# Row exchange of the rotary embedding by DMA instead of a product, with the sine product on GpSimd

## The reference, cut to what matters

```
def apply_rope(x, cos, sin):
    x1, x2 = jnp.split(x.astype(jnp.float32), 2, axis=-1)
    c = cos[None, :, None, :]
    s = sin[None, :, None, :]
    return jnp.concatenate([x1 * c - x2 * s, x2 * c + x1 * s], axis=-1).astype(x.dtype)
```

## Time and profile before

| | us |
|---|---|
| runs (three) | 2032.0, 2032.95, 2035.33 |
| median | 2032.95 |
| profiled execution, its own time | 2036.08 |
| profiled execution, span of the trace | 2034.3 |
| TensorE busy (matmul) | 1961.6, 96% of the span |
| VectorE busy | 1085.8, 53% |
| ScalarE busy | 986.6, 48% |
| GpSimd busy | 753.6, 37% |

### The profile page before, as it was taken

How to read it: one execution, slowest core, us unless ns; L and a number is a source line. 1 busy time by engine, 2 the same in 40 slices (tenths; PEclk the granted TensorE clock), 3 DMA queues, 4 the chain that set the end, 5 groups by cost and what they waited for, 6 DMA issues and landing times.

```text
span 2034.3 us, 25753 instructions
## 1 busy us (share of the span) xinstructions
PE 1961.6 (96%) x10060; PEld 1623.3 (80%) x10060; DVE 1085.8 (53%) x1966; ACT 986.6 (48%) x1731; POOL 753.6 (37%) x341
## 2 busy tenths in 40 slices
PE   6999999999999999999999999999999989999997
PEld 5778888876778777777788888888878888888886
DVE  5376553368664677776737464412536584344214
ACT  5356644366653555555526444422545464444323
POOL 3421243433333333333243444444342334444442
PEclk9999999999999999999999999999999999999999
DMA  5211122211112222222132322333221213322332
GB/s 183 83 43 51 53 77 81 91 52 53 53 53 93 73 73 73 73 73 73 63 103 74 108 95 93 101 89 101 63 62 47 73 59 107 99 98 94 96 93 70
DMA packets 50201, 162.48 MB, mean 80 GB/s; under 512 B 5408, under 2 KB 12192, under 8 KB 49952
## 3 DMA queue, kind: packets, MB, share of 16 engines
q1 hardware_dynamic: 49792, 160.10, 24.9%
q10 hardware_dynamic: 288, 0.74, 0.1%
HBM read 158.72 MB, written 2.10 MB: 79 GB/s over the span
## 4 chain that ended last, share of the span: by engine, by line
PE 80%; DVE 14%; ACT 4%; issue 2%; DMA 0%; POOL 0%; ACTq 0%; DVEq 0%
PE ps L1826 19%; PE ps L1829 19%; PE ps L1827 19%; PE ps L1891 3%; PE ps L1876 2%; PE ps L1838 2%; PE ps L1841 2%; PE ps L1839 2%; DVE tmp L2390 2%; PE ps L1884 2%; DVE s_xbc L2369 1%; PE ps L1860 1%; PE ps L1854 1%; PE ps L1853 1%; PE ps L1851 1%
## 5 line engine op out<-in xcount | busy, mean ns | idle before, releaser
L2565 POOL TENSOR_TENSOR wl<-st,wh 128x1024 fp32r<-128x1024 f32 (+2 forms) x311 | 719.2, 2315 | 1215.1 <-ACT wh L1997 1214.8
L1826 PE MATMUL ps<-xh,wh 128*128 128x512 f32 x1368 | 561.0, 410 | 2.2 <-DVE s_xbc L2369 1.3
L1997 ACT ACTIVATE wh<-st 128x1024 fp32r<-128x1024 f32 (+2 forms) x311 | 314.1, 1010 | 512.6 <-PE ps L1829 450.9
L1829 PE MATMUL ps<-xh,wl 128*128 128x512 f32 x1368 | 534.7, 391 | 0.0
L1827 PE MATMUL ps<-xl,wh 128*128 128x512 f32 x1368 | 533.3, 390 | 0.0
L1826 PEld LDWEIGHTS ps<-xh,wh 128*128 128x128 f32 x1368 | 257.5, 188 | 61.3 <-issue 11.6
L1829 PEld LDWEIGHTS ps<-xh,wl 128*128 128x128 f32 x1368 | 256.9, 188 | 56.3 <-POOL wl L2565 0.8
L1827 PEld LDWEIGHTS ps<-xl,wh 128*128 128x128 f32 x1368 | 257.6, 188 | 52.5 <-issue 6.0
L2524 DVE SCALAR_TENSOR_TENSOR tmp<-ps,vec,tmp 128x510 f32<-128x510 f32 (+1 forms) x176 | 131.3, 749 | 223.4 <-ACT tmp L2176 220.5
L2482 DVE SCALAR_TENSOR_TENSOR res<-res,ps 128x512 f32<-128x512 f32 (+1 forms) x37 | 22.7, 614 | 212.4 <-PE ps L1829 204.7
L1826 PE MATMUL ps<-fa_h,wh 128*128 128x512 f32 x308 | 120.6, 392 | 0.0
(11 more groups left out here) (280 smaller groups left out, 3559.8 us busy)
## 6 DMA issues: line engine op xcount, KB each, us to landing
st<-in_f_up SPq DMA_DIRECT2D x88, 512.0 KB, 3.2
st<-in_s_xbc SPq DMA_DIRECT2D x32, 512.0 KB, 3.5
st<-in_f_dn SPq DMA_DIRECT2D x32, 512.0 KB, 3.5
st<-in_o_fm SPq DMA_DIRECT2D x24, 512.0 KB, 3.5
st<-in_e_fm SPq DMA_DIRECT2D x21, 512.0 KB, 3.6
st<-in_s_z SPq DMA_DIRECT2D x16, 512.0 KB, 3.5
st<-in_s_out SPq DMA_DIRECT2D x16, 512.0 KB, 3.5
st<-in_f_dn SPq DMA_DIRECT2D x16, 384.0 KB, 3.1
```

Source lines behind the costliest of these rows:

```text
L1826: e.matmul(u.bank.ap, hi, x.h[:, kk, :], start=first, stop=False)
L1829: e.matmul(u.bank.ap, lo, x.h[:, kk, :], start=False, stop=last).then_inc(S["mm"], 1)
L1997: e.activation(P.mem["wh"][w.m % NWR][:, 0:w.n], P.mem["stage"][w.m % NSTAGE][:, 0:w.n], ACT.Copy).then_inc(S["w_hi"], 1)
L2565: e.tensor_tensor(P.mem["wl"][w.m % NWR][:, 0:w.n], P.mem["stage"][w.m % NSTAGE][:, 0:w.n], P.mem["wh"][w.m % NWR][:, 0:w.n].bitcast(F32), ...
```

## The change: exchange by DMA, sine on GpSimd, loads as steps of the planner

In `rope_g` the product with the permutation matrix goes away, and with it the PSUM bank that it took. SyncE issues four DMAs of 32 rows by 512 columns (64 KB each) that copy g into the buffer x with the 32-row groups exchanged. They carry one semaphore, `turn0` or `turn1` in turn. GpSimd multiplies x in place by the sine table, where VectorE did so from PSUM. g is held until both GpSimd products are done.

The planner changes too. A turn counts 2000 ns of SyncE. The high and low part of a weight tile count by the tile's width. A weight load counts 550 ns of SyncE, and lands 2950 ns later. The load of tile 3 and later is a step of its own in the planner, which is placed when its staging buffer comes free, and no longer right behind the split of an earlier tile. In the latent attention the second half of the values is projected after the second head's projections (`h == 1`) instead of after the first's.

```diff
     "pe": (..., "blk", "perm", "score", ...
->
     "pe": (..., "blk", "score", ...
-    "dve": (..., "qk_n", "rope_s", "rope_add",
+    "dve": (..., "qk_n", "rope_add",
-    "pool": ("w_lo", "rope_c"),
+    "pool": ("w_lo", "rope_c", "rope_s"),
-           "pos_in", "out"),
+           "pos_in", "out", "turn0", "turn1"),
...
+        self.turns = ring(["turn0", "turn1"])
...
+        if kind in ("w_hi", "w_lo"):
+            return 210 + 0.82 * o[0].n if kind == "w_hi" else 100 + 2.25 * o[0].n
+        if kind[:4] == "w_in":
+            return 550
...
-        w.loaded = self.put(f"w_in{m % NSTAGE}", w, over)
+
+        def bring():
+            w.loaded = yield (f"w_in{m % NSTAGE}", w, over)
+        if m < NSTAGE:
+            w.loaded = self.put(f"w_in{m}", w, over)
+        else:
+            self.start(0, bring(), True)
...
     def rope_g(self, g):
         x = yield from self.taken(self.tmp)
         dst = yield from self.taken(self.tmp)
-        rp = yield from self.taken(self.aux)
-        t = yield ("perm", rp, g, g.ready)
+        way = yield from self.taken(self.turns)
+        t = yield (way.ap, x, g, g.ready, [x.freed, way.freed])
         b2 = yield ("rope_c", dst, g, g.ready, self.rope_ready)
-        b1 = yield ("rope_s", x, rp, t, self.rope_ready)
-        rp.release(b1)
+        b1 = yield ("rope_s", x, t, self.rope_ready)
+        way.release(b1)
         b3 = yield ("rope_add", dst, x, b1, b2)
         x.release(b3)
-        g.release(t, b2)
+        g.release(b2, b1)
...
-            if h == 0:
+            if h == 1:
                 us = yield from values(1)
...
-            e.matmul(rp.ap, P.c(C_PERM), g.ap, start=True, stop=True).then_inc(S["perm"], 1)
...
-            e.tensor_tensor(x.ap, rp.ap, P.c(C_SIN, 512), ALU.mult).then_inc(S["rope_s"], 1)
...
+        elif kind == "rope_s":
+            x, turned, table = o
+            pool.wait_ge(turned)
+            pool.wait_ge(table)
+            e.tensor_tensor(x.ap, x.ap, P.c(C_SIN, 512), ALU.mult).then_inc(S["rope_s"], 1)
...
+        elif kind[:4] == "turn":
+            x, g, ready, freed = o
+            sp.wait_ge(ready)
+            sp.wait_ge(freed)
+            for r in range(0, 128, 32):
+                e.dma_start(x.ap[r ^ 32:(r ^ 32) + 32, :], g.ap[r:r + 32, :]).then_inc(S[kind], 16)
```

More of the change, by code:

```diff
@@ L59 @@
 STEPS = {
-    "pe": ("mm", "mm_half", "mm_tok", "ones", "blk", "perm", "score", "flip", "pv", "feat", "va_t", "dt_t", "cumsum",
+    "pe": ("mm", "mm_half", "mm_tok", "ones", "blk", "score", "flip", "pv", "feat", "va_t", "dt_t", "cumsum",
            "bc_t", "x_t", "cb", "u_mm", "cum_t", "cum_b", "y_mm"),
@@ L65 @@
             "f0", "fsilu", "sine", "lat", "q_in", "v_a", "head_hi", "gate_in", "gate_s"),
[L66 removed]
+    "dve": ("nrm", "split_lo", "v_in", "va_out", "bias_s", "bias_m", "neg_sink", "neg_g", "qk_n", "rope_add",
             "mask", "add_b", "mn", "sink_mn", "flip_d", "sink_x", "sums", "rec", "o_n", "y_g", "res_add", "acc",
@@ L82 @@
 LENGTH = {"pe": 440, "act": 620, "dve": 692, "pool": 1280, "sp": 1300, "actq": 1300}
-LENGTHS = {"mm": 681, "mm_half": 362, "mm_tok": 681, "ones": 857, "blk": 857, "perm": 857, "cumsum": 960, "bc_t": 330, "dt_t": 270,
+LENGTHS = {"mm": 681, "mm_half": 362, "mm_tok": 681, "ones": 857, "blk": 857, "turn0": 2000, "turn1": 2000, "cumsum": 960, "bc_t": 330, "dt_t": 270,
            "cb": 896, "cum_b": 240, "cum_t": 900, "sel": 210, "y_mm": 1750, "w_hi": 1048, "table": 1283, "conv0": 778, "f0": 778, "ln": 680,
@@ L262, in put @@
         self.idle[name] = t - (OVERLAP if name in ("act", "dve") else 0)
-        self.ends[step] = t + (PE_DEEP if name == "pe" else DMA_DEEP if kind in DMA else 0)
+        self.ends[step] = t + (PE_DEEP if name == "pe" else DMA_DEEP + 750 * (kind[:4] == "w_in") if kind in DMA else 0)
         return step
@@ L341, in next_split @@
         if m >= len(self.weights) or (m >= NWR and not self.w[m - NWR].over):
+            return None
+        if m < self.nload and self.w[m].loaded is None:
             return None
@@ L1806, in wait_ge @@
             if place > self.seen.get(of, 0):
-                self.e.wait_ge(self.S[kind], 16 * n if kind in DMA else n)
+                self.e.wait_ge(self.S[kind], (64 if kind[:4] == "turn" else 16) * n if kind in DMA else n)
                 self.seen[of] = place
@@ L1865, in pe_program @@
             e.matmul(st.ap, P.c(C_BLK), s.ap, start=True, stop=True).then_inc(S["blk"], 1)
-        elif kind == "perm":
-            rp, g, ready = o
-            pe.freed(rp)
-            pe.wait_ge(ready)
-            e.matmul(rp.ap, P.c(C_PERM), g.ap, start=True, stop=True).then_inc(S["perm"], 1)
         elif kind == "score":
```

6 lines of the change are left out of this document (removed).

## The result

| | before | after |
|---|---|---|
| median of five runs of each, us | 2032.95 | 2024.32 |
| lowest and highest | 2029.95, 2035.33 | 2022.66, 2027.10 |
| ratio with its 95% interval | | 0.9958 [0.9947, 0.9969] |
| profiled execution | 2036.08 | 2023.36 |
| its span | 2034.3 | 2021.5 |

The account below looks back on a forecast made before the run. TensorE, busy for 96% of the span, was taken as the bound. Products removed (-22.6 us) plus waits at rotated tiles (+3.2) gave -19.4, from 2032.95 to 2013.6, said as 2014 us; own range 2007 to 2019, wider range 2007 to 2026.

Parts of the forecast that it names:

- the first term: On TensorE, removing 26 permutation products of 0.87 us each was to save 22.6 us, all of it on the bound engine.
- that sign: Sign of being right: TensorE's busy time in the three rotation stretches down by about 22 us in all.
- The way of a tile: From the norm's product to the sine product's end, a rotated tile's path grows from 2.15 to 5.0 us (4.0 to 10.0).
- The term of 3.2 us for waits at rotated tiles: TensorE waits 0.2 us at each of 16 places where a score is first to read a rotated tile.
- GpSimd: 26 sine products add 33.3 us to GpSimd; delayed weight tiles and held VectorE products were taken to cost nothing.
- Rival 1: GpSimd's products hold VectorE products before the scores; 0.8 us late at each of 16 places, 12.8 us, so 2023; chance 0.15.
- VectorE's relief: VectorE loses 26 sine products, 18.0 us, worth nothing by itself except where it shortens a TensorE wait.
- SyncE's queue: 104 more DMA issues beside the loads, and loads as planner steps, were taken to cost nothing, 2 us either way.
- Rival 2: Turns come late behind loads in SyncE's queue and land slowly; 16 waits of 3.2 us, so 2062; chance 0.07.
- The chances: For the whole kernel: faster than 2028.9 us 0.86, within 0.2% 0.06, slower 0.08; the forecast itself 0.62.
- Wrong altogether: Sign of complete failure: the whole kernel's span falls by less than 10 us though the products are gone.

Follow-up runs that it names:

- e1: The kernel before in its own order, with 24 of the 26 permutation products replaced by an empty TensorE step: 2025.11 us, ratio 0.9952.
- e2: The changed kernel in its own order without the turn's DMAs, GpSimd's sine product reading the unexchanged g: 2027.37 us, ratio 0.9964 to before.
- e3: The changed kernel in its own order, with GpSimd's sine product over 16 of 512 columns: 2021.25 us, ratio 0.9930 to before.
- e4: The changed kernel with the turn by DMA kept but the sine product back on VectorE, planned anew: 2036.84 us, ratio 1.0012 to before.
- e15: The changed kernel with loads issued the old way up to the odd layer and the cosine product on VectorE, planned anew: 2027.84 us.
- e5: The kernel before with only the planner's part of the change (loads as steps, lengths by width, `h == 1`): 2037.17 us, ratio 1.0013.
- e10: The changed kernel with its new rotation, but loads planned and issued as before and `h == 0`: 2057.97 us, ratio 1.0120 to before.
- e17: The changed kernel with loads issued the old way up to the odd layer and the planner's sine product length 2000, not 1280: 2032.68 us.

## Why the prediction was wrong

**The failed step** is the first term: "So the product costs 1.32 - 0.45 = 0.87 us", 26 x 0.87 = 22.6 us, "All of it lies on the bound engine". The length is right. TensorE's busy time in the three stages fell by 20.3 us (4.0, 10.9 and 5.3), about the 22 foretold (in the fixed stretches of the earlier trace rows it fell by 6.7 only, since other work moved into them, so that sign could not be read there). What was wrong is that all of it lay on the path: 24 products alone bring 9.5 us (e1), 11.4 less than their 20.9, and that is more than the whole shortfall of 10.8 us. The rule given, "work taken off TensorE in these stretches is time taken off the kernel, as long as what it waits for doesn't come later", fails for sixteen products in a stretch in which something else is nearly as late. From 206.08 of 215 us busy and waits of 5.7 us I concluded that little was left to wait for; but the 5.7 us in 8 waits were what showed of a second path, and removal brought out more of it (9.3 in 13, e1; 6.2 us more idle time in the odd stage). Its condition, that what TensorE waits for doesn't come later, was not the point: in e1 nothing comes later, and half is lost all the same. A view that shows the second path is the chain of waits in that stretch. From 480 to 560 us it reads as follows in before, with the softmax's steps by name:

```profile
by line: issue 13.2%; PE ps L1826 10.4%; PE ps L1827 9.9%; PE ps L1829 9.8%; PE ps L1870 6.8%; DVE o_pr L2365 5.1%; DVE small L2276 4.9%; PE ps L1876 4.8%; ACT o_pr L2037 4.8%; PE ps L1891 4.7%; PE ps L1884 4.5%; DVE qz L2537 2.4%; DVE smal
```

Here 15% of the path are the combination, the search and the exponential, and another 13% issue. TensorE's lines that are shown make 51%, where it has 80% of the whole span's chain. The chain alone would not have given the size, since it names one path and not the length of the next.

**The way of a tile**, 2.15 to 5.0 us, grew as forecast: 2.41 + 2.0 + 1.29 = 5.7 us where nothing is in front of it, within the bounds of 4.0 and 10.0. The term of 3.2 us for waits at rotated tiles came out at 2.7 (`kz`), but not for the reason given: without the DMAs 2.4 of it stay and nothing is gained (e2). That its size was right is luck.

**GpSimd**, taken as nothing net: without its long sine products 3 us are gained (e3), and the mechanism, held VectorE products, is in the chain at 418.94 us. "GPSIMD Engine Reference" of the Trainium skill, section Key points, says that VectorE instructions with two SBUF inputs contend with GpSimd. The trace agrees, and the measured price is 6.2 us of VectorE in the odd stage, half of it in the combinations of the probabilities. Rival 1 named this mechanism, and put it at the wrong place and size: its 12.8 us of waits at tiles are some 3.

**VectorE's relief** was 9.3 us of its busy time (1085.8 to 1076.5) and not 18.0, since GpSimd held other products of it. It was taken as nothing and is probably worth something: giving its sine products back costs 12.5 us (e4), giving it the cosine products 5.7 (e15), in orders of their own. e1 keeps VectorE's sine products and lacks this gain. So the change may have it in addition to the products' 9.5 us and spend it on GpSimd's products, the planner's part and the clock. That balance is not shown: of the kernels with a part of the change only e1, e2 and e3 keep a given order.

**SyncE's queue**, taken as nothing with 2 us either way: right for the change as it stands, and wrong as a statement on its planner's part. I took the loads as steps of the planner for a matter of rows. Together with the lengths and `h == 1` they are worth +3 us without the turn (e5) and -34 us with it (e10 against the change). Rival 2 had one link of the mechanism; that its 2062 is near e10's 2058 is luck, since it counted sixteen waits of 3.2 us, and e10 has one of 11.2, other idle time and a lower clock.

**The chances.** 0.86 for faster was right. 2024 us is about the time of rival 1 (2023, given 0.15), but its reason explains 3 of the 10.8 us of shortfall. That the time fell into the range up to 2026 is therefore no success of the mechanism. "Wrong altogether: the span falls by less than 10 us though the products are gone" gives no clear answer: 12.8 us in the profiles, 8.6 in the medians.

## What to carry to other kernels

A busy share of 96% says that an engine has little room, not that work taken from it is gained in full. If 16 equal pieces go, ask of each what else would be last there, and read it from the chain of waits in that stretch; doubling and removing the same instruction (17.9 us against 9.5 here) measures it in two runs. Where each experiment gets an order of its own, 10 us of difference can be the order (e17), so those in the order of a known kernel are the ones to build on. Where a transfer joins a queue with loads, the queue's order is part of the change: the same DMAs brought the kernel to 8.6 us under before or to 23.5 us over it, by the order that the planner gave.

## What the runs showed of the hardware

- A VectorE product with two inputs in buffers took 2.09 and 1.65 us instead of 0.69 while GpSimd ran instructions of 2.73 and 1.70 us; each ended 0.55 us after GpSimd's. Summed over the odd stage, 16 sine products of 1.29 us on GpSimd held VectorE for 6.2 us (e3).
- A DMA of 64 KB from buffer to buffer, 32 rows of 2 KB, takes 0.59 us of issue, more than the 0.33 us of a load of 128 rows in the same queue (at 1519.82 in e10), and lands in 2.0 us, up to 3.8.
- TensorE's wait of 11.2 us was followed by 10 us at a granted clock of 0.50, its lower level of 1.2 GHz (e10). There 128x512 products started 0.43 to 0.53 us apart (at 1543 us), and 0.23 apart at the full clock (at 1546.3). Shorter stretches at the lower level come and go: in after the mean clock was 0.83 from 580 to 600 us, which is 6.8 us at the lower level, where TensorE had been idle for 1 us of the 5 before it fell. Such a stretch costs at most half its length, 3.4 us here.
